# Moving head group C's cache halves to other units of a hybrid decoder step, and reading three sequences of it in whole page rows

## The reference, cut to what matters

```python
kc_all = jnp.concatenate([paged_rows(cache_c_k), kc], axis=1)     # past of C, by page table
vc_all = jnp.concatenate([paged_rows(cache_c_v), vc], axis=1)
oc = diff_attend(qc, kc_all, vc_all, q_pos, lam_l, lam_init, subln_g_l, rel_bias)
o = jnp.concatenate([oa, ob, oc], axis=-1)                        # A, B, C side by side
```

## Time and profile before

| | |
|---|---|
| Runs (median of 3) | 1348.69 us (1345.12 to 1351.5) |
| The profiled execution | 1345.06 us, span of its instructions 1343.3 us |
| PE busy (share of span) | 1283.9 us (96%) |
| DVE, ACT busy | 495.4 us, 265.4 us |
| Mean granted clock of PE | 0.986 |
| Queue q1 (SP) | 156192 packets, 345.62 MB |
| Queue q10 (ACT) | 34506 packets, 16.74 MB |

### The profile page before, as it was taken

The page is one execution under the profiler, slowest core; times in us unless marked ns, Lnnn a source line. Parts: engine busy times, 40 slices in busy tenths (PEclk is TensorE's granted clock), DMA queues, the critical chain, the costliest instruction groups (busy, mean ns, idle before and its releaser), DMA issues.

```text
span 1343.3 us, 23207 instructions
## 1 busy us (share of the span) xinstructions
PE 1283.9 (96%) x8038; PEld 806.7 (60%) x8038; DVE 495.4 (37%) x1433; ACT 265.4 (20%) x683; POOL 59.6 (4%) x265
## 2 busy tenths in 40 slices
PE   6989999979999999999999999999899999999998
PEld 3544356645657666666656444665556577767775
DVE  1203568866672111011040065878566411101113
ACT  0111145322123111000023112543221401100001
POOL 1000011101001000000010000001000100000000
PEclk8999999998999999999999999999999999999999
DMA  9899899999874587978754687999996365676663
GB/s 373 245 319 272 294 325 353 337 347 353 292 257 143 203 293 243 354 241 314 290 203 158 217 300 253 363 369 351 349 353 226 141 219 198 243 261 219 214 211 139
DMA packets 190814, 363.83 MB, mean 271 GB/s; under 512 B 23072, under 2 KB 141608, under 8 KB 189034
## 3 DMA queue, kind: packets, MB, share of 16 engines
q1 hardware_dynamic: 156192, 345.62, 74.6%
q10 hardware_dynamic: 34506, 16.74, 4.7%
HBM read 354.20 MB, written 58.40 MB: 307 GB/s over the span
## 4 chain that ended last, share of the span: by engine, by line
PE 71%; SPq 15%; issue 4%; DMA 4%; DVE 3%; ACT 1%; DVEq 1%; ACTq 0%
PE psf L1148 23%; PE psf L1623 21%; SPq L556 13%; PE psf L1526 4%; PE psf L1169 3%; PE psf L1607 3%; DMA ring<-in_tiles 2%; PE psf L1465 2%; PE psf L1397 2%; PE psf L1350 2%; PE psf L1199 2%; SPq L566 1%; DMA big<-in_pool_cv 1%; PE psf L1232 1%; PE psf L1521 1%
## 5 line engine op out<-in xcount | busy, mean ns | idle before, releaser
L1148 PE MATMUL psf<-hT,ring 128*128 128x320 f32 x1184 | 324.5, 434 | 3.8 <-DMA ring<-in_tiles 3.6
L1148 PEld LDWEIGHTS psf<-hT,ring 128*128 128x128 f32 x1184 | 223.4, 190 | 106.8 <-issue 13.5
L1623 PE MATMUL psf<-big,ring 128*128 128x320 f32 x1024 | 278.0, 433 | 2.1 <-DVE big L2113 2.1
L1623 PEld LDWEIGHTS psf<-big,ring 128*128 128x128 f32 x1024 | 194.0, 190 | 86.6 <-issue 4.2
L2113 DVE TENSOR_TENSOR big<-sq 128x320 f32<-128x320 f32 x64 | 31.5, 492 | 239.1 <-ACT sq L1117 238.9
L1723 DVE TENSOR_SCALAR rstd<-psf,adaT 128x256 f32<-128x256 f32 x40 | 19.3, 481 | 236.1 <-PE psf L1623 232.0
L1117 ACT ACTIVATE sq<-psf 128x320 f32<-128x320 f32 x64 | 28.1, 438 | 231.8 <-PE psf L1148 220.8
L1074 ACT ACTIVATE sq<-xT 128x320 f32<-128x320 f32 x32 | 15.0, 470 | 289.8 <-DVE xT L1736 276.6
L1397 PE MATMUL psf<-big,ptbuf 128*32 128x128 f32 x2048 | 64.7, 280 | 6.4 <-DMA big<-in_pool_cv 6.4
L1350 PE MATMUL psf<-big,qs 128*32 128x512 f32 x512 | 66.4, 614 | 3.8 <-DMA big<-in_pool_bk 3.0
L1397 PEld LDWEIGHTS psf<-big,ptbuf 128*32 128x32 f32 x2048 | 56.1, 112 | 13.0 <-issue 11.2
(11 more groups left out here) (219 smaller groups left out, 1355.4 us busy)
## 6 DMA issues: line engine op xcount, KB each, us to landing
ring<-in_tiles SPq DMA_DIRECT2D x246, 512.0 KB, 4.5
big<-in_cache_a SPq DMA_DIRECT2D x64, 768.0 KB, 7.0
out_cache_a<-in_cache_a SPq DMA_DIRECT2D x64, 768.0 KB, 5.6
big<-in_pool_bk SPq DMA_DIRECT2D x128, 192.0 KB, 6.4
big<-in_pool_bv SPq DMA_DIRECT2D x128, 192.0 KB, 7.0
big<-in_pool_cv SPq DMA_DIRECT2D x192, 64.0 KB, 5.8
big<-in_tiles SPq DMA_DIRECT2D x22, 512.0 KB, 7.7
big<-in_pool_ck SPq DMA_DIRECT2D x128, 64.0 KB, 4.6
```

Of the source, the lines that this page charges most:

```text
L1148: ins = pe.matmul(ps[:, 0:T], ring[:, s, k, :], rhs[:, k, :], start=k == 0, stop=k == KD - 1)
L1623: ins = pe.matmul(bank[6 + m % 2][:, 0:T], ring[:, s, k, :], uT[:, KD * q + k, :], start=q + k == 0, stop=q == 3 and k == KD - 1)
```

## The change

- Units 0 to 7 take C of sequence `c = n % 4`, first half in units 0 to 3 and second half in 4 to 7. Units 8 to 15 take C of sequence `c = n // 2` with half `n % 2`: two neighbours share a sequence.
- For the last three sequences (units 10 to 15, `whole`) ACT reads each page once with its full rows of 1024 bytes, 8 transfers of 128 KB for the keys and 8 for the values of a pair. The keys are issued at the end of ACT's units 7, 9, 11, the values at the end of 8, 10, 12. They lie alternately in the C parts of both unit buffers and in space of `hT`, `zT`, `workbuf` and `wkibuf`. SP issues no C for those units.
- `sbias[h]` now goes with C's half `h`. It holds A's rows in units 0 to 7 and B's rows in 8 to 15, so that they are read again in each layer: B's by ACT (`load_rows`, three transfers of 16 rows of 4128 bytes in its unit 3, three in unit 6), and A's for the second layer by SP in the first layer's MLP. DVE waits for them in units 8, 9 and, in the second layer, 0 and 4.
- Where `u.c != u.b` (units 4 to 14) `turn_far` has one more small transpose. `place_outputs` has four small copies instead of two.

```diff
+        self.c, self.half = (n % 4, n // 4) if n < NB else (n // 2, n % 2)
+        self.whole, self.store = n >= NB + 2, n // 2 % 2
...
+        def bias_rows(h):
+            return bass.AP(dist_s.tensor, h * NDIST + NT - 1, [[NDIST, 2], [H * NDIST - 1, NT], [1, L]])
...
-                    load_c(l, then, was, 1, range(NPG // 2 if then.second else NPG))
+                    if then.second and not then.whole:
+                        load_c(l, then, pages(then.c, CHECKED), 1, range(NPG // 2))
+                    elif not then.second:
+                        load_c(l, then, was, 1)
...
+                        if l + 1 < DEPTH and d in (10, 12):
+                            load_rows(d // 2 - 5)
...
+                def load_whole(pool, places, signal, at):
+                    for j in range(NPG):
+                        act.dma_start(places[j // (NPG // 2)][:, j % (NPG // 2), :],
+                                      pool[ds(at[j] + l * N_PHYS, 1)].rearrange("o p w -> (o p) w")).then_inc(signal, 16)
...
+                def load_rows(e):
+                    for g in range(3):
+                        act.dma_start(sbias[e][G * g:G * g + 2 * NT, :], bias_rows(HA + 2 * g)).then_inc(ld_rows[e], 16)
...
+                    if u.n + 1 in (4, 7):
+                        load_rows(u.n // 6)
...
+                    then = UNIT[u.n + 3] if u.n in (7, 9, 11) else None
+                    if then:
+                        at = pages(then.c, CHECKED)
+                        if u.n == 7:
+                            act.wait_ge(tile_used, used(MID[l][-1]))
+                        act.wait_ge(u_s.sem, u_s.done(l, u.n))
+                        load_whole(a["pool_ck"], whole_k[then.store], ld_wk[then.store], at)
+                    then = UNIT[u.n + 2] if u.n in (8, 10, 12) else None
+                    if then:
+                        if u.n == 8:
+                            act.wait_ge(sel_set.sem, sel_set.done(l, 0))
+                        act.wait_ge(u_o.sem, u_o.done(l, u.n - 1))
+                        load_whole(a["pool_cv"], whole_v[then.store], ld_wv[then.store], at)
...
+                    if u.c != u.b:
+                        zc = TS - NT - NT * u.c
+                        pe.transpose(bank[2][0:TS, 352:384], znew[3 * G:P, zc:zc + TS], ident[3 * G:P, 3 * G:P])
...
+                    if u.n in (NB, NB + 1):
+                        dve.wait_ge(ld_rows[u.half], 48 * (2 * l + 1))
+                    elif l and u.n in (0, 4):
+                        dve.wait_ge(ld_rows[u.half], 48 * 2 * l)
...
-                        ins = dve.tensor_copy(oT[q, u.o:u.o + 4, t0:t0 + NT],
-                                              bass.AP(first.tensor, first.offset, [list(first.ap[0]), [2 * NT, 4], [1, NT]]))
+                        part = bass.AP(first.tensor, first.offset, [list(first.ap[0]), [2 * NT, 3], [1, NT]])
+                        dve.tensor_copy(oT[q, u.o:u.o + 3, t0:t0 + NT], part)
+                        ins = dve.tensor_copy(oT[q, u.oc, tc:tc + NT], bank[3][q, P + NT * (6 + half):P + NT * (7 + half)])
```

More of the change, by code:

```diff
@@ L277, in program @@
                  for i, m in enumerate(PARTS.values())}
+        flat = lambda x: x[:, :, :].rearrange("p k t -> p (k t)")
+        four = KD * P
+        whole_k = [[fours(kv[:, s, CK_AT:CK_AT + four]) for s in range(2)],
+                   [fours(flat(hT)[:, 3 * P * len(PARTS):3 * P * len(PARTS) + four]), fours(flat(zT[:, QI:QI + 4, :])[:, 0:four])]]
+        whole_v = [[fours(kv[:, s, CV_AT:CV_AT + four]) for s in range(2)],
+                   [fours(workbuf[:, 0:four]), fours(wkibuf[:, 0:four])]]
         ik = [x[:, 0:PAST].rearrange("p (j w) -> p j w", j=NPG)
@@ L354, in program @@
         ld_dist = sem("ld_dist")
+        ld_wk = [sem(f"ld_wk{s}") for s in range(2)]
+        ld_wv = [sem(f"ld_wv{s}") for s in range(2)]
+        ld_rows = [sem(f"ld_rows{e}") for e in range(2)]
         st_dist = sem("st_dist")
@@ L573, in load_c @@
             def load_c(l, u, at, half, which=range(NPG)):
-                load_pages(l, at, a["pool_cv" if half else "pool_ck"], P * u.second, (ck_in, cv_in)[half][u.s],
+                load_pages(l, at, a["pool_cv" if half else "pool_ck"], P * u.half, (ck_in, cv_in)[half][u.s],
                            (ld_ck, ld_cv)[half][u.s], which)
@@ L584, in load_bias @@
                     sp.dma_start(sbias[e][at:at + NT, :],
-                                 bass.AP(dist_s.tensor, n * row + NT - 1, [[H * NDIST - 1, NT], [1, L]])).then_inc(ld_dist, 16)
+                                 bass.AP(dist_s.tensor, h * row + NT - 1, [[H * NDIST - 1, NT], [1, L]])).then_inc(ld_dist, 16)
                 elif n < HA + HB + 2 * HC:
@@ L683, in _ @@
                     then, after = UNIT[u.n + 2], UNIT[u.n + 3] if u.n + 3 < UNITS else None
-                    at, was = pages(after.b, CHECKED) if after else None, at
+                    at, was = pages_of(after) if after else None, at
                     if after:
@@ L1026, in place_outputs @@
                         first = bank[3][q, P + NT * half:P + NT * half + NT]
-                        ins = act.activation(oT[q, u.o:u.o + 4, t0:t0 + NT],
-                                             bass.AP(first.tensor, first.offset, [list(first.ap[0]), [2 * NT, 4], [1, NT]]),
-                                             ACT.Copy)
+                        part = bass.AP(first.tensor, first.offset, [list(first.ap[0]), [2 * NT, 3], [1, NT]])
+                        act.activation(oT[q, u.o:u.o + 3, t0:t0 + NT], part, ACT.Copy)
+                        ins = act.activation(oT[q, u.oc, tc:tc + NT], bank[3][q, P + NT * (6 + half):P + NT * (7 + half)], ACT.Copy)
                     ins.then_inc(u_out.sem, 1)
@@ L1333, in logits @@
                         pe.wait_ge(z_set.sem, z_set.done(l, NZ - 1))
+                    if u.n == 4:
+                        pe.wait_ge(z_set.sem, z_set.done(l, MADE_AT[KC + 1]))
                     keys_wait(u)
-                    t0 = TP + NT * u.b
+                    t0, tc, of = TP + NT * u.b, TP + NT * u.c, slice(P * u.half, P * u.half + P)
                     for q in range(3):
@@ L1392, in values @@
                                 lhs = PT[:, j, G * c:G * c + G]
[L1393 removed]
+                                rhs = (v_in[u.s][:, j, P * c:P * c + P] if c < 3
+                                       else whole_v[u.store][j // 4][:, j % 4, P * u.half:P * u.half + P] if u.whole
+                                       else cv_in[u.s][:, j, :])
                             else:
```

56 lines of the change are left out of this document (33 added, 23 removed).

## The result

The changed kernel takes 1359.54 us (median of 5 runs, 1356.61 to 1361.62) against 1346.17 us for the kernel before on the same chip: ratio 1.0094, 95% interval 1.0068 to 1.0119, some 13 us slower (9.2 to 16.0 from the interval). The profiled execution has 1361.29 us and a span of 1359.4, where before had 1345.06 and 1343.3 (+16.1 in the span), at nearly the same mean clock of PE (0.983 and 0.986).

A forecast was written before the change was run, and what follows sets the result against it. It took PE and the DMA engines as both near full, with transfers setting the pace until unit 11's values. 9.5 us a layer, twice, less 1.3 gave +17.7, rounded to 17: 1345 + 17 = 1362 us, own range 1353 to 1370, overall 1341 to 1370.

The forecast's parts named there:

- The case that I called likeliest: Whole kernel: 1362 us, with the bias rows on two already full DMA engines as largest term; chance 0.58.
- Two engines, 7.7 us a layer less 1.3 once, 14.1 in all: ACT's units 3 and 6: bias rows go to two full engines, 7.7 us a layer; the first layer absorbs 1.3 once.
- the signs: Right if values of units 5 to 8 begin waiting, 7 to 11 no shorter; wrong if unit 8 at 279 as before.
- Whole pages, +0.5 a layer: C of units 10 to 15: 2.0 us more bytes before unit 11's values against 1.5 us fewer packets, net +0.5 a layer.
- ACT's issues cost 0: End of ACT's units: 72 C transfers issued instead of 96, where ACT then waits for DVE: 0 us.
- The terms add: Sum over a layer: 7.7 + 0.5 + 1.0 + 0.3 = 9.5 us; two layers less 1.3 give +17.7.
- `place_outputs`, +1.0 us a layer: DVE, units 12, 13 and 15: two more copies add some 0.35 us without slack, 1.0 us a layer (0 to 1.8).
- The sign that I named: PE's transpose behind `place_outputs` (`PE L1382`) would wait some 0.3 us for DVE `oT`.
- The transposes, 0.3 a layer: PE: each extra transpose costs 0.1 us, counted on three uncovered units, 0.3 us a layer.
- SP's rows in the MLP, 0: SP's six `load_rows` in the MLP are covered by four ring places ahead of PE: 0 us.
- The clock: Units 9 to 12: a low clock could come more or less often and move some us either way.
- the faster rival, SP's issuing as the bound: SP's issuing, not the engines, is short: units 7 to 11 near 42 us, total 1336; chance 0.16.

The follow-up runs named there:

- halves: The changed kernel with C of units 10 to 15 read in halves of 512 bytes again, by ACT and SP as before; 1360.68 us, ratio 1.0114.
- rowstwice: The changed kernel with every bias row that ACT reads again read twice, the second time into rows no query uses; 1378.30 us, ratio 1.0232.
- norows: The changed kernel without re-reading the bias rows and without DVE's waits for them; 1350.99 us, ratio 1.0041.
- before_turns: The kernel before with only the extra small transpose in units 4 to 14 added; 1345.56 us, ratio 0.9999.
- rows8_early: The changed kernel with bias rows in transfers of 8 rows and the first whole keys issued at the end of ACT's unit 6; 1353.05 us, ratio 1.0052.
- noturn: The changed kernel without bias re-reads and extra transposes, first whole keys issued at the end of ACT's unit 6; 1346.36 us, ratio 1.0001.
- rows8: The changed kernel with each bias re-read as six transfers of 8 rows instead of three of 16; 1354.96 us, ratio 1.0064.
- before_rows: The kernel before with only B's bias rows read again over themselves in ACT's units 3 and 6; 1359.92 us, ratio 1.0113.

## Why the prediction was right

The forecast, 1362, stands beside 1359.54 measured and 1361.29 in the profiled execution. The case that I called likeliest is the one that happened, and its large term is shown by the runs. That the sum comes so near is in part luck, as the smaller steps show. By its own steps:

- **Two engines, 7.7 us a layer less 1.3 once, 14.1 in all.** Right in mechanism, and near in size. The packets give 18 for each transfer and run two at a time, and the rows alone cost 14.7 us on the kernel before. The price of a row was too low: 169 ns came from a line far beyond its three points, and the traces have 204, so two engines are busy for 9.8 us a layer and not for 8.1. Not all of that is felt. The first layer takes less, 6.6 against 8.9 us by sections, which fits the reason that I gave (it is less full) but doesn't prove it. Of the signs, 7 to 11 is no shorter and the values of unit 8 come at 283.6 and not at 279. That the values of units 5 to 8 begin to wait was too much: only unit 7 does in both layers, and unit 8 in the first, where it waited before too.
- **Whole pages, +0.5 a layer.** Not contradicted, and too small to be tested: halves and the changed kernel can't be told apart. That the bytes before unit 11 decide is not shown, since PE's waits in the three places of the first whole keys are of three kinds.
- **ACT's issues cost 0.** The working of this step was wrong. I counted that ACT issues fewer transfers over a layer and did not look where they stand. In unit 6 it has three more (2.3 us) ahead of keys that PE needs next. With eight more there PE waits 3.15 us for `turned_unit`, and with three more transfers of rows (rowstwice) it waits 5.33 us for `zT`. In the changed kernel itself no wait of PE's is put down to them.
- **The terms add.** This was taken for granted and fails. The rest of the change without the rows (norows) costs 4.9 us (2.4 to 8.6 from the interval), where my terms give 1.0 + 2.0 + 0.6 = 3.6; the rows alone cost 14.7 (12.8 to 17.5); both together cost 13.4 (9.2 to 16.0) and not 19.6. The wait for the first whole keys, which I had not named, is the likeliest place where they overlap.
- **`place_outputs`, +1.0 us a layer.** Too high. The four copies and PE behind them in unit 12 of the second layer:

```profile
1003.28 0.17 DVE L2045 COPY oT<-psf 64x24 f32<-64x24 f32 x1
1003.37 0.15 DVE L2046 COPY oT<-psf 64x8 f32<-64x8 f32 x1
1003.53 0.19 DVE L2045 COPY oT<-psf 64x24 f32<-64x24 f32 x1
1003.64 0.16 DVE L2046 COPY oT<-psf 64x8 f32<-64x8 f32 x1
```

```profile
1002.17 0.27 PE L1444 MATMUL psf<-ident,znew 128*64 128x128 f32 x1
1002.37 0.21 PE L1447 MATMUL psf<-ident,znew 32*64 32x32 f32 x1
1002.51 0.43 PE L1482 MATMUL psf<-turnO,osb 128*128 128x64 f32 x2
...
1004.20 0.66 PE L1458 MATMUL psf<-ident,S 128*128 128x128 f32 x4
```

  The copies overlap one another and need 0.52 us instead of 0.38, not 0.35 more; PE comes 0.40 us after the last, without a wait. The reading that no slack was left was wrong already in the rows of before, where PE comes to that transpose without a pause, 0.20 us behind the copies. Units 12 to 15 grow by 0.5 and 0.8 us, and before_turns, which has no extra copy, grows by 0.7 and 0.7. So the copies cost nothing that can be seen. The sign that I named, PE's transpose waiting some 0.3 for DVE's `oT` in these units, did not come.
- **The transposes, 0.3 a layer.** The price of one was too low and the count too. The rows above have the next instruction 0.14 us behind the small one, and a step between units grows from 11.2 to 11.5 us, 10.4 to 10.7, 10.9 to 11.3: about 0.3 each. So the last units did not keep their length, as I had named for a sign. Under the waits for transfers most of it vanishes, so that on the kernel before they come to at most 2.4 us in all; my 0.6 is within that.
- **SP's rows in the MLP, 0.** Nothing speaks against it: from the values of unit 15 to those of unit 0 of the second layer it is 476.2 us, where before has 475.6.
- **The clock.** The prediction left it out of the sum and said that it could move some us either way. It fell, from 0.97 and 0.96 to 0.90 between units 7 and 11 in both layers, in the stretch where PE waits.

So the sum of 17 was 13.4 in the medians and 16.1 between the profiled executions. The large term was right; the 2 us of copies were not there, the small terms seem to lie partly under the large one, and the start at 1345, some 1 us under the median of before in its runs, made up for a part of that. The near hit of 1362 on 1359.54 is such a sum of misses and not only a measure of the mechanism.

What stays open: the faster rival, SP's issuing as the bound, would have shown units 7 to 11 near 42 us, and no complete version did (44.6 at best, in rows8_early). noturn's 4.6 us rests on intervals that touch. What the 4.9 us of norows consist of is not shown, nor what part of the rows' price comes by way of the clock. That two engines and not the bytes make the price is shown by the packets and by rows8 (4.6 us less for the same bytes); a split over all 16 engines was not tried.

## What to carry to other kernels

Look at how many engines a small transfer is spread over before putting it into a stretch where all are full: its rows stand on those few engines ahead of every transfer that needs all of them. Look also at what the issuing engine has to do behind the transfers: its issues take longer when the engines are full, and its arithmetic comes after them. When moving a transfer to another queue or place only renames PE's wait (C's keys, ACT's copy, B's keys) and leaves the time, the cause is not found yet. Costs that fall into one another's lag need not add: put the disputed part alone into the kernel before, since taking it out of the changed one may measure it less what lay beneath. And read the granted clock of each stretch, not only its mean over the kernel, before calling a longer stretch a longer wait.

## What the runs showed of the hardware

- The packet count of a queue tells the spread: 18 packets for 16 rows is two engines (at most three, mostly two of them run at a time in the trace), 16 packets for 8 rows (rows8: 27978 - 27594 = 384 for 24 transfers) is eight (up to seven at a time).
- A row of 4128 bytes takes 204 ns on average where two engines carry them all, and 240 to 249 ns where eight do; the shortest take 160.
- Twelve transfers of 66 KB, 0.8 MB in all, cost 14.7 us on full queues of the kernel before, and twelve more in the changed kernel 18.8 us; at the 340 GB/s of that stretch their bytes are 2.3 us.
- An issue is 0.34 to 0.6 us of the issuing engine's time, some 0.5 from one to the next, and 1.10 to 1.24 for the first of a bias group. Eight of SP's took 8.46 us behind the rows and 4.59 without them; seven of ACT's took 3.62 behind three transfers of rows and 9.14 behind six.
- A transpose of 32x32 takes 0.21 us of PE and sets a unit back by about 0.3 where PE doesn't wait, nearly as much as one of 128x128 at 0.27.
- The granted clock of units 7 to 11 lay between 0.87 (rowstwice, first layer) and 0.98 (noturn). At 0.90 PE was busy for 43.5 us in before_rows, first layer, where the kernel before, with the same work for PE, has 40.8 us at 0.97.
